# RWKV-7 scan of a two-layer backbone: four 64x64 quadrants per product, T's transpose through the identity, masks at the eviction of X, keys made per segment

## What is computed

```python
def rwkv_scan(r, decay, k, v, kk, a, s0):
    def step(s, inp):
        rt, wt, kt, vt, kkt, at = inp
        sa = jnp.einsum('bhvk,bhk->bhv', s, -kkt)
        s = s * wt[:, :, None, :] + sa[..., None] * (kkt * at)[:, :, None, :] + vt[..., None] * kt[:, :, None, :]
        return s, jnp.einsum('bhvk,bhk->bhv', s, rt)
...
        for d in range(2):
            w = -jax.nn.softplus(-(w0[d] + jnp.tanh(xw @ w1[d]) @ w2[d]).astype(f32)) - 0.5
            a = jax.nn.sigmoid(a0[d] + (xa @ a1[d]) @ a2[d])
            kd = k * (1.0 + (a - 1.0) * k_a)
            per_dir.append((jnp.exp(-jnp.exp(heads(w))), heads(kd), heads(a)))
```

## Time and profile before

| | us |
|---|---|
| median of three runs | 3103.59 |
| lowest and highest | 3097.29, 3108.31 |
| profiled execution, its time | 3107.18 |
| profiled execution, its span | 3105.3 |
| scan of the context, 1111.05 to 1343.28 | 232.23 |
| scan of the latent tokens, 1494.43 to 1766.27 | 271.84 |

### The profile page before, as it was taken

How to read it: one execution, slowest core, us unless ns; L and a number is a source line. 1 busy time by engine, 2 the same in 40 slices (tenths; PEclk the granted TensorE clock), 3 DMA queues, 4 the chain that set the end, 5 groups by cost and what they waited for, 6 DMA issues and landing times.

```text
span 3105.3 us, 73377 instructions
## 1 busy us (share of the span) xinstructions
PE 2796.5 (90%) x33759; PEld 2012.9 (65%) x33760; DVE 732.0 (24%) x1200; ACT 457.5 (15%) x809; POOL 46.8 (2%) x147
## 2 busy tenths in 40 slices
PE   6998798999997888879898877999999999999993
PEld 2653533444442688867788757877869696968772
DVE  1122513000002456643556641000000000100001
ACT  3231112000002322241222112000000000000001
POOL 0000003000000000000000000000000000000000
PEclk8988898999998899989999887999999999999996
DMA  6216027222224000032000214888888797888880
GB/s 221 82 55 244 1 68 266 82 68 81 80 69 149 28 2 3 4 123 77 3 4 4 66 68 160 316 312 320 300 331 300 291 347 279 321 302 319 308 294 14
DMA packets 178946, 493.68 MB, mean 159 GB/s; under 512 B 9362, under 2 KB 73188, under 8 KB 172500
## 3 DMA queue, kind: packets, MB, share of 16 engines
q1 hardware_dynamic: 176852, 482.73, 43.6%
q0 software_dynamic: 1792, 6.19, 0.7%
HBM read 487.84 MB, written 1.05 MB: 157 GB/s over the span
## 4 chain that ended last, share of the span: by engine, by line
PE 80%; DVE 11%; issue 4%; ACT 3%; DMA 1%; SPq 0%; POOL 0%; DVEq 0%; ACTq 0%; POOLq 0%
PE banks L933 22%; PE banks L949 12%; PE banks L709 10%; PE banks L784 9%; PE banks L577 9%; PE banks L719 5%; DVE ring_arena L1531 4%; PE banks L619 2%; PE banks L516 1%; PE banks L906 1%; DVE rstd L1243 1%; PE banks L918 1%; PE banks L864 1%; PE banks L671 1%; DMA ring_arena<-in_mod_w 1%
## 5 line engine op out<-in xcount | busy, mean ns | idle before, releaser
L933 PE MATMUL banks<-ring_arena 128*64 128x112 f32 x14336 | 694.0, 259 | 0.0
L933 PEld LDWEIGHTS banks<-ring_arena 128*64 128x64 f32 x14336 | 687.1, 137 | 8.8 <-issue 8.0
L784 PE MATMUL banks<-ring_arena 64*64 64x64 f32 x13312 | 437.4, 223 | 64.6 <-DVE ring_arena L1531 62.5
L784 PEld LDWEIGHTS banks<-ring_arena 64*64 64x64 f32 x13312 | 426.3, 140 | 71.1 <-DVE ring_arena L1531 67.0
L949 PE MATMUL banks<-ring_arena 128*112 128x512 f32 x896 | 385.8, 592 | 0.0
L577 PE MATMUL banks<-ring_arena 128*128 128x256 f32 (+1 forms) x1024 | 316.1, 472 | 21.7 <-ACT ring_arena L993 12.7
L709 PE MATMUL banks<-ring_arena 128*128 128x512 f32 x704 | 305.3, 597 | 0.0
L949 PEld LDWEIGHTS banks<-ring_arena 128*112 128x112 f32 x896 | 158.0, 177 | 221.9 <-issue 221.9
L577 PEld LDWEIGHTS banks<-ring_arena 128*128 128x128 f32 x1024 | 200.2, 196 | 138.5 <-issue 97.3
L1697 DVE TENSOR_TENSOR ring_arena<-ring_arena,banks 128x448 f32<-128x448 f32 x32 | 19.9, 621 | 1034.1 <-PE banks L933 1034.1
L709 PEld LDWEIGHTS banks<-ring_arena 128*128 128x128 f32 x704 | 134.8, 192 | 169.7 <-issue 169.7
(11 more groups left out here) (262 smaller groups left out, 1683.2 us busy)
## 6 DMA issues: line engine op xcount, KB each, us to landing
ring_arena<-in_moe_w_gu SPq DMA_DIRECT2D x256, 896.0 KB, 5.4
ring_arena<-in_moe_w_d SPq DMA_DIRECT2D x112, 1024.0 KB, 7.0
ring_arena<-in_mod_w SPq DMA_DIRECT2D x48, 1024.0 KB, 7.1
ring_arena<-in_ff_w_gu SPq DMA_DIRECT2D x22, 1024.0 KB, 5.1
ring_arena<-in_rw_w_rkv SPq DMA_DIRECT2D x20, 1024.0 KB, 11.1
ring_arena<-in_gla_w_in SPq DMA_DIRECT2D x12, 1024.0 KB, 5.3
ring_arena<-in_ff_w_d SPq DMA_DIRECT2D x11, 1024.0 KB, 4.9
ring_arena<-in_gla_w_out SPq DMA_DIRECT2D x4, 1024.0 KB, 13.8
```

The lines of the kernel that those rows point to most:

```text
L784: ins = T.matmul(bank[d][b][r, p * CH:p * CH + CH], lhs[r, p, :], EYE2[r, :] if rhs is None else rhs[r, p, :], start=(q == 0), stop=(q == ...
L933: ins = T.matmul(bank[CH * h:CH * h + CH, (c % 4) * CAP:(c % 4) * CAP + CAP], w[:, kk, c * P + CH * h:c * P + CH * h + CH], XG[:, 2 * kp + ...
```

## The change

- **Quadrants.** `swapped` replaces `heads`: the head pairs 0 to 3 go through the two quadrants as before (rows r to columns r), the pairs 4 to 7 through the other two (rows r to columns 1 - r) and into another bank, in turn. The two halves of a pair thus land on each other's partitions in the output, and every operand is laid out so that each product finds its halves. `home` keeps all eight pairs in the two quadrants of before (TXT5), and `home_and_swapped` starts a sum of terms so and goes on in the other order (W, y).
- **Levels.** X is the product with NT, the whole of N's transpose copied once by ACT; DVE evicts X and multiplies it by the mask of its level, which now holds -1 (L1597). T gains TX on DVE (L1602); TT is made by a product of T with the identity and an ACT copy, except at level 5. The five masked copies NT1 to NT5 go; N and its transpose are two products.
- **Keys per segment.** `directions` makes the keys of both directions, and the rates times the normalised keys, once ahead of each segment: 16 TENSOR_SCALAR of 128x4x64 and four TENSOR_TENSOR of 128x2048. U1 is then an add and one step for each pair.
- **Front.** B, K, R and PC of the next chunk (`front`, L1642 to L1646) stand behind level 5 and ahead of the adds of y and ST; R and PC get two buffers. `sums` moves from behind level 2 to behind level 1. The exponentials are spread over levels 2 to 4. YY lies elsewhere, and its fill comes behind the latent segment's first front.

```diff
-                def heads(d, b, terms, need):
...
+                def head(d, pair, half, p, lhs, rhs, home, start, stop):
+                    bank = ps[4 * d + 2 * pair + p // 4]
+                    col = 256 * half + CH * (p % 4)
+                    for r in range(2):
+                        o = r if home or p < 4 else 1 - r
+                        ins = T.matmul(bank[rows[o], col:col + CH], lhs[rows[r], p, :],
+                                       EYE2[rows[r], :] if rhs is None else rhs[rows[r], p, :],
+                                       start=start, stop=stop, skip_group_check=True)
+                    return ins
+
+                def swapped(d, pair, half, terms, need):
+
+                    wait_for(d, need)
+                    for p in range(4):
+                        for q, (lhs, rhs) in enumerate(terms):
+                            for g in range(2):
+                                ins = head(d, pair, half, p + 4 * g, lhs, rhs, False, p == 0 and q == 0, q == len(terms) - 1)
+                    ins.then_inc(pe_s[d], 1)
...
                 for d in both:
-                    heads(d, 3, [(VT[:, i if d == 0 else SC - 1 - i], None)], [])
+                    pe.wait_ge(pre_v[d], 3 * (SC * lat + i) + 3)
+                    if lat and i:
+                        pe.wait_ge(dv_s[d], done[d] - 2)
+                    swapped(d, 0, 0, [(w[d]["B"], A[d])], [(FRS, "B")])
+                    swapped(d, 0, 1, [(VT[:, i if d == 0 else SC - 1 - i], None)], [])
                 for d in both:
-                    heads(d, 0, [(w[d]["B"], A[d])], [(DVS, "B")])
-                    heads(d, 1, [(w[d]["K"], A[d])], [(DVS, "K")])
+                    if i:
+                        pe.wait_ge(dv_s[d], done[d] - 1)
+                    swapped(d, 1, 0, [(A[d], w[d]["B"])], [])
+                    swapped(d, 1, 1, [(w[d]["K"], A[d])], [(FRS, "K")])
...
-                for l in levels:
+                for l in range(1, 5):
                     for d in both:
-                        if l == 1:
-                            heads(d, 0, [(w[d]["NT1"], w[d]["T"])], [(DVS, "NT5"), (ACS, "T0")])
-                        else:
-                            heads(d, 0, [(w[d][f"NT{l}"], w[d]["T"])], [(DVS, f"T{l - 1}")])
+                        swapped(d, 1, 0, [(w[d]["TT"], w[d]["X"])], [(DVS, f"X{l}"), (ACS, "Bt" if l == 1 else f"TT{l - 1}")])
...
-                        if l < 5:
-                            heads(d, 1, [(w[d]["TT"], w[d]["X"])], [(ACS, f"X{l}")] + ([(DVS, f"TT{l - 1}")] if l > 1 else []))
-                            heads(d, 2, [(w[d]["X"], w[d]["TT"])], [])
-                        else:
-                            heads(d, 2, [(w[d]["X"], w[d]["TT"])], [(ACS, "X5"), (DVS, "TT4")])
+                        swapped(d, 1, 1, [(w[d]["T"], None)], [(DVS, f"T{l}")])
+                        swapped(d, 0, 0, [(w[d]["NT"], w[d]["T"])], [(ACS, "Kt")])
                 for d in both:
-                    pe.wait_ge(dv_s[d], DVS.before(lat, i))
-                    heads(d, 3, [(A[d], w[d]["ST"]), (w[d]["Lak"], w[d]["Vt"])], [])
+                    home(d, 1, 0, w[d]["X"], w[d]["TT"], [(DVS, "X5"), (ACS, "TT4")])
...
+            def directions(sg):
...
+                dve.wait_ge(S["pj_out"], KEY_PJ[sg] + HP)
+                for dst, a in ((KD[0], AA[0]), (KD_TMP, AA[1])):
+                    for p in range(HP):
+                        k = VEC["rw_k_a"] + p
+                        ins = Vv.tensor_scalar(dst[:, :, p, :], a[:, :, p, :], vecs[:, k:k + 1], KAM[:, p:p + 1], ALU.mult, ALU.add)
+                link(ins)
+                Vv.tensor_tensor(flat(KD[0]), flat(KD[0]), flat(KEY), ALU.mult)
+                link(Vv.tensor_tensor(flat(AA[0]), flat(AA[0]), flat(KK), ALU.mult))
+                Vv.tensor_tensor(flat(KEY), flat(KEY), flat(KD_TMP), ALU.mult)
+                link(Vv.tensor_tensor(flat(AA[1]), flat(AA[1]), flat(KK), ALU.mult))
...
+                for l in range(1, 6):
                     for d in range(2):
-                        if l < 5:
-                            add(d, w[d]["T"], w[d]["T"], bk(d, 1), (PES, f"TX{l}"))
-                        add(d, w[d]["TT"], w[d]["TT"], bk(d, 2), (PES, f"TXT{l}"))
-                    if l == 2 and i < SC - 1:
-                        sums(SC * lat + i + 1)
+                        mult(d, by_bank(w[d]["X"]), scan_bank(d, 0, 0), over(LM[l][1 - d]), (PES, f"X{l}"))
+                    for d in range(2):
+                        t = by_bank(w[d]["T" if l < 5 else "TT"])
+                        add(d, t, t, scan_bank(d, 1, 0), (PES, f"TX{l}" if l < 5 else "TXT5"))
+                    if l == 1 and i < SC - 1:
+                        sums(g)
                     if l == 3 and i < SC - 1:
-                        removal(SC * lat + i + 1)
+                        removal(g)
+                if i < SC - 1:
+                    front(g)
...
+            def front(g):
+                lat, i = g // SC, g % SC
+                for d in range(2):
+                    w = WORK[d]
+                    dve.wait_ge(pre_s[d], 3 * g + 3)
+                    if i:
+                        dve.wait_ge(pe_s[d], PES.value(lat, i - 1, "Kt"))
+                    Vv.tensor_tensor(w["B"], pick(AA[d], d, g), w["e3"], ALU.mult).then_inc(fr_s[d], 1)
+                    Vv.tensor_tensor(w["K"], pick(KD[d], d, g), w["e3"], ALU.mult).then_inc(fr_s[d], 1)
+                    if lat:
+                        Vv.tensor_tensor(w[f"R{i % 2}"], pick(RR, d, g), w["e2"], ALU.mult).then_inc(fr_s[d], 1)
+                    Vv.tensor_copy(PC[i % 2][d], w["e2"][:, :, CH - 1 if d == 0 else 0]).then_inc(fr_s[d], 1)
```

More of the change, by code:

```diff
@@ new lines, in swapped, with home @@
+                def swapped(d, pair, half, terms, need):
[5 more added lines that the diff above has]
+                    ins.then_inc(pe_s[d], 1)
+                def home(d, pair, half, lhs, rhs, need):
+                    wait_for(d, need)
+                    for p in range(HP):
+                        ins = head(d, pair, half, p, lhs, rhs, True, p % 4 == 0, True)
+                    ins.then_inc(pe_s[d], 1)
@@ L782, in heads, with home_and_swapped @@
+                def home_and_swapped(d, pair, half, name, first, terms, need):
+                    wait_for(d, need)
+                    for p in range(4, HP):
+                        ins = head(d, pair, half, p, *first, True, p == 4, False)
+                    ins.then_inc(pe_s[d], 1)
+                    for p in range(4):
+                        head(d, pair, half, p, *first, True, p == 0, False)
+                    wait_for(d, [(PES, name)])
+                    for p in range(4):
                         for q, (lhs, rhs) in enumerate(terms):
[L783 to L786 removed]
+                            for g in range(2):
+                                ins = head(d, pair, half, p + 4 * g, lhs, rhs, False, False, q == len(terms) - 1)
```

201 lines of the change are left out of this document (97 added, 104 removed).

## The result

| | before | after |
|---|---|---|
| median, us | 3103.38 (4 runs) | 3035.65 (4 runs) |
| lowest and highest | 3097.29, 3108.31 | 3033.42, 3040.57 |
| ratio, 95% interval | | 0.9781 (0.9764 to 0.9799) |
| profiled execution: time, span | 3107.18, 3105.3 | 3034.87, 3032.8 |
| scan of the context | 232.23 | 203.26 |

A forecast was written before the change was run, and what follows sets the result against it. PE was taken to bound the inverse's levels, DVE each chunk's head. From the profiled 3107.18 us, scan -180.5, U1 -6.9 and clock +14 gave 2934; the runs' median lying 3.6 lower, the forecast was 2930 us, range 2905 to 3020.

The forecast's parts named there:

- Four quadrants, P = 0.47: Scan products: four quadrants overlap at 14.6 ns per MATMUL, so a swapped product lasts P = 0.47 us, a home one 0.93.
- Rival B: Scan products: the instruction stream sets a floor between 14.6 and 29.2 ns per MATMUL; 2950 to 3020 us; chance 0.17.
- rival C: Scan products: diagonal quadrants don't overlap, a product stays 0.93 us; 3062 us at most, 3048 without clock cost; chance 0.06.
- The level of 3.6 us: Each level of the inverse: from six products, 5.6 us, PE-bound, to a chain of waits of 3.6 us; four such 14.4.
- tail and head: Chunk's work after the levels and from the last U to X1: 8.7 us each in context; latent 12.4 and 10.1.
- Sums, 3.1 us a chunk on the path: DVE's sums (L1495, L1499) behind level 1: 3.4 us, of which 3.1 delay the next level, which needs DVE for X.
- Front hidden: Next chunk's six DVE steps behind level 5: 4.7 us of work beside 6 of W and SA, so no cost.
- Keys per segment hidden: DVE ahead of each segment: 14.8 us more work, covered by 20.97 and 29.60 us of idle time.
- U1 -6.9: DVE chain behind the scan (L1605 to L1619): 12.3 us becomes one add and eight STT, 5.5 us, saving 6.9.
- The clock, +14: Scan: PE idle in new heads and sums brings half-clock stretches, one a chunk, costing 14 us; bounds 0 and 40.
- Rival D: Scan products: changing quadrant pairs drains the array, 0.09 us per change, a product 1.66 us; about 3350 us; chance 0.04.
- 16 P and 10 to 17 P: Swapped-product times per chunk, in levels and in tail plus head; each 0.1 us more adds 3.3 us a chunk, 26 in all.

The follow-up runs named there:

- the first stream: Changed kernel with 512 wait-free products (64x64 by 64 columns, four quadrants) put ahead of the scan on PE: groups of 128 MATMULs every 3.46 to 3.74 us.

## Why the prediction was wrong

- **Four quadrants, P = 0.47: the step that failed.** The array does run four quadrants at once, 14.7 ns per MATMUL inside a group. As an average of a long stretch it is 29.1, and P is 0.93. The row I used against a bound of the feed, four MATMULs that started within 0.05 us, was a burst behind a wait; the prediction said so itself and let it count. The row that sustained rates rest on, 640 MATMULs at 29.2 ns, fitted the array's time in two quadrants and was taken for it alone. In the trace before, the instruction queue's row for the 37.5 us from 1193.45 on reads:

```profile
q8 instruction: 10, 0.16, 2.0%
```

  That is one transfer in 3.75 us, as long as PE took for 128 MATMULs. It couldn't be told from a limit, but it was the number to ask about, since the change was to double the rate.
- **Rival B had the cause, and too little weight.** Its band ended at 3020, between four quadrants' rate and rival C's. The measured rate is at its slow end, and so the time, 3036, is nearest to C's (3048 without a clock cost), by B's mechanism. The 25 ns per matmul of the Trainium skill ("TensorE: Matmul & The Clock Gate", section "Wait — 56ns, not 53.3ns?") is not what binds: inside a group MATMULs start every 14.7 ns. Its estimate, 3016, came close for another reason.
- **The chains.** The level of 3.6 us, tail and head are borne out in sum as a lower bound: with half of each product the schedule gave 276 us and the chip took 278.8. In the changed kernel they are covered: a context chunk takes 1664 x 29.1 ns = 48.4 us (47.9 and 50.5 from sums to sums) and not 35.7, a latent one 57.5 and 59.9 and not 40.8.
- **Sums, 3.1 us a chunk on the path**: hidden behind the feed (3032.4 when split). **Front hidden**: right, PE waits for it only at the two segments' starts; moved back it costs some 9 or 10 us, at the edge of the noise.
- **Keys per segment hidden, U1 -6.9**: right, 6.62 and 17.61 us of idle time are left, and U1 gained 6.8. What the keys bring in the chunks is small once the front is hidden, some 4 us of 33.
- **The clock, +14**: wrong in sign. The granted clock in the scans is 0.98 and 0.96, where it was 0.94. In two quadrants, where PE's work is the bound, that gave back some 18 us (worked out below). With half of the instructions it fell to 0.82: the cost is there when PE waits for the other engines, and the pauses of the feed didn't bring it.
- **Rival D**, draining at each change of pair: nothing of it. Groups of 128 change pairs all through at 14.7 ns.
- **Two slips that decided nothing.** 16 P and 10 to 17 P are 26 to 33 P a chunk, so 0.1 us on P adds 24 us in all and not 26; the times of B and C come out up to 11 us too late. And of the 62.5 us of waits put down to the heads of the chunks, 13.6 stood at the segments' starts (two of 6.78).

What the gain is made of, by the run with two quadrants: PE's idle time in the two scans fell from 66.7 us (504.1 less 437.4 busy) to 22.1 (456.8 less 434.7), the two waits at the segments' starts staying (13.6 and 16.9 us): 44.6 less. 512 MATMULs more at 29.8 ns cost 15, but a MATMUL took 29.8 ns of PE's busy time instead of 31.1, 18 us less, with a granted clock of 0.98 instead of 0.94; that the clock is the reason is an estimate from these rows. Together 47 off the scans, and U1 gives 7: 54, where the times give 53 to 56. The quadrants add 12 to 15.

## What to carry to other kernels

When a change lets an engine do its instructions faster, ask how fast they arrive: count recorded instructions per us in the longest stretch without a gap, and the transfers of the instruction queue beside it. A stretch in which an engine is full and its instruction transfers follow each other at a steady period may stand at two bounds at once, and a burst behind a wait shows only what was stored. Past that point fewer and larger instructions pay and faster ones don't: joining two products of one stationary matrix gave 20 us in four quadrants and nothing in two.

## What the runs showed of the hardware that I had not expected

- PE's instructions came in groups of 256 recorded ones (128 MATMULs and 128 weight loads), with one transfer of 16 KB for each, every 3.46 to 3.74 us without any wait in the stream, every 3.5 to 4.0 between full groups of the scan and 3.8 on average: 27 to 31 ns per MATMUL with its load. The transfer itself is short: 51 of them take 1.8% of 16 engines' time in 193.7 us, 1.1 us each on an average. What fills the rest of the period wasn't tried and stays open, and so does why the period varies.
- Some 236 MATMULs can be ready behind a wait and then go at the array's rate: they took 3.71 us in the first stream.
- Four 64x64 quadrants run at once: 14.7 ns per MATMUL of 64 columns, 58 in one quadrant.
- 16 moving columns were no faster than 64 when the weights have 64 columns: 14.6 ns in four quadrants, in the one full group that ran at the full clock.
- Four quadrants with 128 columns took about 27 ns per MATMUL for 24 us at the full clock, without a pause.
